# Two feed-forward units multiplied block by block at the entry, and weight conversions and norm sums reordered

## The reference

```python
def rmsnorm(x, g):
    xf = x.astype(jnp.float32)
    y = xf * lax.rsqrt(jnp.mean(xf * xf, axis=-1, keepdims=True) + RMS_EPS)
    return (y * g.astype(jnp.float32)).astype(x.dtype)

def swiglu_2(x, w_gu, w_down):
    gu = x @ w_gu
    gate, up = gu[..., :D_FF], gu[..., D_FF:]
    return (jax.nn.silu(gate) * up) @ w_down
...
        x = x + rmsnorm(m, mix_norm_post[l])
        f = swiglu_2(rmsnorm(x, ffn2_norm_pre[l]), ffn2_w_gu[l], ffn2_w_down[l])
        x = x + 0.5 * rmsnorm(f, ffn2_norm_post[l])
```

## Time and profile before

| what | value |
|---|---|
| median of 3 runs | 3744.84 us (3740.54 to 3745.47) |
| the profiled execution's own time | 3738.52 us |
| its span | 3736.9 us |
| mean granted PE clock | 0.969 |
| start of the entries of stages 3, 5, 7, 9 | 1087.4, 1931.1, 2643.3, 3350.3 us |

### The profile page before, as it was taken

The page is one execution under the profiler, slowest core; times in us unless marked ns, Lnnn a source line. Parts: engine busy times, 40 slices in busy tenths (PEclk is TensorE's granted clock), DMA queues, the critical chain, the costliest instruction groups (busy, mean ns, idle before and its releaser), DMA issues. The chain is left out here.

```text
span 3736.9 us, 45677 instructions
## 1 busy us (share of the span) xinstructions
PE 3495.2 (94%) x18504; PEld 2736.0 (73%) x18510; DVE 2004.4 (54%) x2653; ACT 1123.5 (30%) x1462; POOL 154.0 (4%) x128
## 2 busy tenths in 40 slices
PE   7999999999999999948699999989999989899998
PEld 6887776688878886838468886765788866567886
DVE  5667546522353335897554335697433348954334
ACT  2222334322232223223232223326322232442222
POOL 0000000000000000000000000330000012300000
PEclk8999999999999999969799999999999999999999
DMA  6544221122222222200012222220222221102221
GB/s 229 183 180 170 89 94 45 60 98 101 90 79 98 93 102 76 102 23 4 1 46 101 101 92 80 86 70 15 87 92 99 98 83 68 57 35 92 99 98 71
DMA packets 47213, 325.58 MB, mean 87 GB/s; under 512 B 5232, under 2 KB 5488, under 8 KB 8672
## 3 DMA queue, kind: packets, MB, share of 16 engines
q1 hardware_dynamic: 41792, 290.04, 21.7%
q0 software_dynamic: 5280, 33.52, 2.5%
HBM read 321.44 MB, written 2.10 MB: 87 GB/s over the span
## 5 line engine op out<-in xcount | busy, mean ns | idle before, releaser
L1914 PE MATMUL PS<-HH,WH 128*128 128x512 f32 x2264 | 900.2, 398 | 50.3 <-DVE HL L2300 42.3
L1916 PE MATMUL PS<-HH,WL 128*128 128x512 f32 x2264 | 885.1, 391 | 0.0
L1915 PE MATMUL PS<-HL,WH 128*128 128x512 f32 x2264 | 884.7, 391 | 0.0
L2282 DVE TENSOR_TENSOR WL<-RAW,WH 128x2048 fp32r<-128x2048 f32 x264 | 613.7, 2325 | 502.0 <-ACT WH L2140 496.4
L2140 ACT ACTIVATE WH<-RAW 128x2048 fp32r<-128x2048 f32 x264 | 503.1, 1906 | 327.5 <-PE PS L1916 319.4
L1914 PEld LDWEIGHTS PS<-HH,WH 128*128 128x128 f32 x2264 | 427.2, 189 | 165.8 <-issue 62.3
L1915 PEld LDWEIGHTS PS<-HL,WH 128*128 128x128 f32 x2264 | 427.4, 189 | 90.6 <-issue 4.6
L1916 PEld LDWEIGHTS PS<-HH,WL 128*128 128x128 f32 x2264 | 426.8, 189 | 90.7
L1914 PE MATMUL PS<-AH,WH 128*128 128x512 f32 x1056 | 412.3, 390 | 3.3 <-DVE A L2348 3.0
L1915 PE MATMUL PS<-AL,WH 128*128 128x512 f32 x1056 | 411.4, 390 | 0.0
L1916 PE MATMUL PS<-AH,WL 128*128 128x512 f32 x1056 | 411.3, 389 | 0.0
(11 more groups left out here) (376 smaller groups left out, 3696.8 us busy)
## 6 DMA issues: line engine op xcount, KB each, us to landing
RAW<-in_w SPq DMA_DIRECT2D x264, 1024.0 KB, 4.8
E<-in_ada POOLq DMA_DIRECT2D x28, 1024.0 KB, 5.1
E<-in_ada SPq DMA_DIRECT2D x4, 1024.0 KB, 11.7
G<-in_ada SPq DMA_DIRECT2D x4, 1024.0 KB, 19.3
X<-in_x SPq DMA_DIRECT2D x1, 2048.0 KB, 13.7
out_x<-A SPq DMA_DIRECT2D x8, 256.0 KB, 2.1
G<-in_cos POOLq DMA_DIRECT2D x4, 256.0 KB, 3.3
G<-in_sin POOLq DMA_DIRECT2D x4, 256.0 KB, 3.6
```

What stands on the lines that cost most here:

```text
L1914: nc.tensor.matmul(out, wh, xh, start=start, stop=False)
L1915: nc.tensor.matmul(out, wh, xl, start=False, stop=False)
L1916: return nc.tensor.matmul(out, wl, xh, start=False, stop=stop)
L2282: nc.vector.tensor_tensor(WL[:, w % 2, :], RAW[:, w % 2, :], WH[:, w % 2, :].bitcast(F32), ALU.subtract).then_inc(w_lo, 1)
```

## The change

- Stages 3 and 5: `entry` gives way to `entry_pair`, which multiplies units 0 and 1 together, in an order (unit, chunk) written out; six of the eight norm products go, VectorE adds the squares of seven chunks (six additions, behind the last low half), and `norm_added` stands ahead of the last two blocks. VectorE's conversion of unit 1 moves ahead of chunk 4's term.
- Stages 7 and 9: unit 1's conversion moves ahead of the norm on ScalarE and VectorE; `norm_added` moves from behind unit 0 to the middle of unit 1.
- In the deferred stages PE's wait ahead of unit u >= 2 is for `up_scaled` instead of `act_ready`.
- `keep_clock` has 9 products instead of 6 ahead of stages 3 and 5.
- `add_squares` and `norm_added` take an order; counts of `sq` follow.

```diff
@@ -1960,14 +1960,14 @@
                 if j == n - 1:
                     last.then_inc(stat_done, 1)
 
-            def norm_added():
+            def norm_added(order=ORDER):
 
                 e = t.add("norms")
                 t.add("sq", KD)
                 pe.wait_ge(sq_added, t.add("added"))
-                nc.tensor.matmul(PS[4 + e % 2][:], ONES[:], SQ[:, ORDER[0], :], start=True, stop=False)
+                nc.tensor.matmul(PS[4 + e % 2][:], ONES[:], SQ[:, order[0], :], start=True, stop=False)
                 pe.wait_ge(sq_done, t("sq"))
-                nc.tensor.matmul(PS[4 + e % 2][:], ONES[:], SQ[:, ORDER[-1], :], start=False, stop=True).then_inc(stat_done, 1)
+                nc.tensor.matmul(PS[4 + e % 2][:], ONES[:], SQ[:, order[-1], :], start=False, stop=True).then_inc(stat_done, 1)
 
             def keep_clock(n):
 
@@ -2003,22 +2003,42 @@
                     for c in range(2):
                         last = mm3(PS[c][:], wh[:, KD * c + k, :], wl[:, KD * c + k, :], xh[:, k, :], xl[:, k, :],
                                    n == 0, n == KD - 1)
-                    if n == KD - 1:
+                last.then_inc(w_used, 1)
+
+            def entry_pair(w, s):
+
+                order = [(0, 0), (0, 1), (0, 2), (1, 0), (0, 3), (1, 1), (0, 4), (1, 2), (1, 3), (0, 5), (1, 4), (0, 6), (1, 5),
+                         (0, 7), (1, 6), (1, 7)]
+                pe.wait_ge(x_done, KD * (s - 1) + 2)
+                for u, k in order:
+                    if k == 0:
+                        unit_arrives(w + u)
+                    if u == 0:
+                        pe.wait_ge(hl_done, t("hl") - KD + k + 1)
+                    if (u, k) == (1, 0):
+                        pe.wait_ge(x_done, KD * (s - 1) + 4)
+                    if (u, k) == (1, 6):
+                        norm_added(entry_order(s))
+                    wh, wl = blocks(w + u)
+                    for c in range(2):
+                        last = mm3(PS[2 * u + c][:], wh[:, KD * c + k, :], wl[:, KD * c + k, :], HH[:, k, :], HL[:, k, :],
+                                   k == 0, k == KD - 1)
+                    if k == KD - 1:
                         last.then_inc(w_used, 1)
-                    if post:
-                        norm(part=(n,))
-                if not post:
-                    norm_added()
 
             def ffn(sub, s):
                 w, base = t("w"), t("act_ready")
                 with_ada = plan["ada"] and s == 0
 
-                def gate_up(u, i=0):
+                scaled = t.add("scaled", KF) - KF if deferred(s) else 0
+
+                def gate_up(u, i=0, between=lambda c: None):
                     unit_arrives(w + u, i)
-                    if u >= 2:
+                    if u >= 2 and deferred(s):
+                        pe.wait_ge(up_scaled, scaled + u - 1 + i)
+                    elif u >= 2:
                         pe.wait_ge(act_ready, base + u - 1 + i)
-                    project(w + u, (2 * (u % 2), 2 * (u % 2) + 1), first=u == 0, xs=halves(s))
+                    project(w + u, (2 * (u % 2), 2 * (u % 2) + 1), first=u == 0 and not deferred(s), between=between, xs=halves(s))
                     if with_ada and 2 <= u < KF - 4:
                         ada(ADA_FIRST + u - 2, i)
                     elif with_ada and u >= KF - 4:
@@ -2026,11 +2046,14 @@
                             ada(a - 2)
 
                 t.add("hl", KD)
-                if deferred(s):
+                if deferred(s) and plan["subs"][s - 1]["post"]:
+                    entry_pair(w, s)
+                elif deferred(s):
                     entry(w, s)
+                    gate_up(1, between=lambda c: c == 0 and norm_added(entry_order(s)))
                 else:
                     gate_up(0)
-                gate_up(1)
+                    gate_up(1)
                 with pe.Fori(0, KF - 6, 4) as i:
                     for u in (2, 3, 4, 5):
                         gate_up(u, i)
@@ -2108,7 +2131,7 @@
                     out_projection(K_ORDER.get(sub["kind"], list(range(KD))))
                 if sub["post"]:
                     norm_added()
-                    keep_clock(6)
+                    keep_clock(9 if deferred(s + 1) else 6)
                     t.add("y_evac", len(post_copies(s)))
                 if plan["ada"] and s == 0:
                     pe.wait_ge(y_evac, t("y_evac"))
@@ -2166,6 +2189,8 @@
                     act.wait_ge(x_done, t("x") - KD + n + 1)
                     nc.scalar.activation(halves(s)[0][:, m, :], X[:, m, :], ACT.Copy, scale=col(plan["subs"][s]["pre"], m)).then_inc(hh_done, 1)
                     nc.scalar.activation(SQ[:, m, :], X[:, m, :], ACT.Square).then_inc(sq_done, 1)
+                if not plan["subs"][s - 1]["post"]:
+                    split(t("w") + 1)
                 rsqrt()
 
             def high(src, shift=None, given=0, ready=lambda m: None, order=range(KD), part=range(KD)):
@@ -2265,8 +2290,11 @@
                         split(t("w") + 1)
                         enter(s + 1) if deferred(s + 1) else norm_in(range(KD))
                     else:
-                        enter(s + 1) if deferred(s + 1) else norm_in(ORDER)
-                        split(t("w") + 1)
+                        if deferred(s + 1):
+                            enter(s + 1)
+                        else:
+                            norm_in(ORDER)
+                            split(t("w") + 1)
 
 
         @block.vector
@@ -2405,13 +2433,13 @@
                 t.add("w", DOWN)
                 t.add("ah", DOWN)
 
-            def add_squares(j):
+            def add_squares(j, order=ORDER):
 
                 if j < 1:
                     return
                 dve.wait_ge(sq_done, t("sq") + j + 1)
-                first = SQ[:, ORDER[0], :]
-                ins = nc.vector.tensor_tensor(first, first, SQ[:, ORDER[j], :], ALU.add)
+                first = SQ[:, order[0], :]
+                ins = nc.vector.tensor_tensor(first, first, SQ[:, order[j], :], ALU.add)
                 if j < KD - 2:
                     chain(ins)
                 else:
@@ -2489,7 +2517,7 @@
                         if m in copied:
                             nc.vector.tensor_copy(Y[:, m, :], PS[m][:]).then_inc(y_evac, 1)
                         add_squares(j)
-                    t.add("sq", 2 * KD)
+                    t.add("sq", KD)
                     t.add("y_evac", len(copied))
                     rsqrt()
                     dve.wait_ge(y_evac, t("y_evac"))
@@ -2510,8 +2538,13 @@
                         ready = following
                         if lo and m >= 1:
                             lo(m - 1)
+                        if lo and m == 3:
+                            split(t("w") + 1)
                     if lo:
                         lo(KD - 1)
+                        for j in range(1, KD - 1):
+                            add_squares(j, entry_order(s + 1))
+                    t.add("sq", KD)
                 else:
                     lo = enter(s + 1) if deferred(s + 1) else None
                     for j, m in enumerate(ORDER):
@@ -2532,12 +2566,12 @@
                     dve.wait_ge(ada_used, ADA)
                     modulation(2 * (ADA - ADA_SLOTS), VECTORS * KD)
                 if s + 1 < len(plan["subs"]):
+                    if deferred(s + 1):
+                        rsqrt()
+                        continue
                     if sub["post"]:
                         split(t("w") + 1)
-                    if deferred(s + 1):
-                        rsqrt()
-                    else:
-                        norm_in(plan["subs"][s + 1]["pre"], plan["subs"][s + 1]["shift"])
+                    norm_in(plan["subs"][s + 1]["pre"], plan["subs"][s + 1]["shift"])
                     if not sub["post"]:
                         split(t("w") + 1)
                 elif plan["final"]:
```

## The result

The changed kernel takes 3750.4 us (median of 15 runs, 3747.17 to 3755.53), the kernel before 3741.6 us (15 runs, 3736.09 to 3746.12): ratio 1.0024, 95% interval [1.0016, 1.0031], so 6 to 12 us slower, 9 in the middle. Forecast were +4.5 us and 3749.3 in a range of 3741 to 3757. The time is in the range and the sign is the forecast's. The size is twice the forecast: it lies just beyond the 0.2% up to which I had put 0.75 of the chance, and outside the +1 to +7 us of outcome D, to which I had given 0.65. That the forecast time is off by only 1.1 us is luck: the median of three runs that it starts from, 3744.8, is 3.2 us above that of the fifteen, and the change was forecast 4.3 us too small.

A forecast was written before the change was run, and what follows sets the result against it. TensorE, busy 94%, was taken as the bound. Stages 3 and 5 +5.2, stages 7 and 9 -9.0, cold clock behind the new gaps +8.3: +4.5 us on 3744.84, so 3749.3 us, range 3741 to 3757.

The forecast's parts named there:

- outcome D: The forecast itself as an outcome for the whole kernel: +1 to +7 us, chance 0.65.
- The pair: Stages 3 and 5: unit 2 starts 2.6 us later each, behind a new gap of 6.8 us; together +5.2 us.
- Stages 7 and 9: Their entries: unit 1's conversion hidden, a gap of 4.1 us at unit 2; -3.8 us in stage 7, -5.2 in 9.
- The clock behind the gaps: TensorE's lowered clock after the four new gaps ahead of unit 2: together +8.3 us, bounds 6.1 and 11.9.
- a value between: Clock cost taken behind each 4.1 us gap, in stages 7 and 9: 1.9 us.
- Rival C: Cold clock decides, on the slow side: 2.98 us at each gap gives +8.1, falls in both pairs +11.3; chance 0.2.
- The advice of the Trainium skill: Leave the clock ramp out of the model as under 1% of a typical span; the sum would be -3.8 us.
- Earlier loads: Loads follow the low halves: unit 3's may start some 8 to 10 us sooner, into an idle queue; worth 0.
- the order of banks: New block order in the pair changes banks each block, as unit 0 did already; worth 0.
- the six additions on VectorE: Stages 3 and 5: adding squares takes 4.3 us in idle time of 6.16, done 3.3 us ahead of PE.
- The relaxed wait: Later units wait on the scaled operand, not the product, about 3 us earlier; PE has no gap there, worth 0.
- within 0.2%: Whole time within 0.2% (7.5 us) of the kernel before: chance 0.75.

The follow-up runs named there:

- x3: Changed kernel with unit 2's conversion moved ahead of the norm on ScalarE and VectorE; ratio 0.9977 to the kernel before.
- x9: Changed kernel with the norm products of stages 3 and 5 two blocks earlier; ratio 1.0009 to the kernel before.
- x8: Changed kernel with products that nobody reads laid in the gaps ahead of unit 2, 7 in stages 3 and 5, 4 in 7 and 9; ratio 0.9998 to before.
- x1: Changed kernel with the old entry and 6 clock-keeping products in stages 3 and 5; ratio 0.9994 to the kernel before.
- x10: Changed kernel with 6 clock-keeping products again, in place of 9, ahead of stages 3 and 5; 3749.64 us in one execution.
- x4: Changed kernel with the norm behind unit 0 again in stages 7 and 9, unit 1 still converted early; ratio 0.9993 to the kernel before.
- x12: Kernel before with 6 products that nobody reads added in the middle of stage 3's feed-forward; ratio 1.0017 to the kernel before.
- x7: Changed kernel with old entry and 9 clock-keeping products in stages 3 and 5, norm behind unit 0 in 7 and 9; 3720.75 us, ratio 0.9948 to before.

## Why the prediction was right, and where it was not

- **The pair.** Forecast: U2 at 33.2 us behind the entry's start, behind a gap of 6.8. Measured 33.3 and 6.68. Each step in between held: the conversion of U1 pushes the fourth low half (1101.55 here, 8.36 us behind the first; before, 6.15), the ten blocks run through, the added squares are there (1112.76) 3.3 us ahead of PE. The step that decides, that the chain from Ln to U2's low half isn't edited and only two blocks are left to cover it, is shown from both sides: x3 moves U2's conversion ahead of the chain and the wait for it is gone, x9 moves the chain 2.7 us ahead and the gap shrinks by as much.
- **Stages 7 and 9.** Forecast: a gap of 4.1 at U2 for one of 6.3 at U1, U1's conversion hidden. Measured 3.96 and 3.97. The net gain was forecast at 1.9 and 3.3 us and is 1.9 and 2.2 (means of two traces each).
- **The clock behind the gaps, the term that was mis-sized.** I took 2.25 us behind the long gaps and 1.9 behind the short ones, together 8.3. Against x8 the changed kernel's two traces give about 2.2 behind 6.7 us, and on the mean 2.4 behind 4.0, together 9.2. The gaps of 4.0 in stages 7 and 9 of x1, x9 and x10 widen the sample: their cost is 1.5 to 1.7 or 2.5 to 2.8, in the mean of all ten 2.1, so "a value between" was not far off, and what a single one costs can't be forecast. Without the clock the sum was -3.8; x8, with the gaps filled, has -3.0. The two differences, 0.9 and 0.8, make the entries +6.2 and not +4.5. Rival C, all four at 2.98 and falls in the pairs, is not what happened, though the whole, +9.0, lies in its range; x10 shows that a fall at the pair's start has no price.
- **A row misread.** The 0.68 of stage 9 is the granted clock in the gap itself (3363.00 to 3369.34), not behind it; no term used it.
- **The advice of the Trainium skill** (TensorE: Matmul & The Clock Gate, Part 1: The HAM clock gate) to leave the ramp out would have given -3.8. Filling the gaps took 9 us of entry length and about 10 of the whole: here that term has the size of the whole change. The page also says that the number of slow products at a kernel's start varies from run to run; in the cost of a gap the traces show such a variation too (stage 7: 2.5 and 1.5 us).
- **The rest, some 3 us.** The whole time is 9.0 above before, the entries' sum 6.2; the interval reaches down to 6.0. All seven timed variants of the changed kernel lie 1 to 5 us above their entries' sums, and for x3, x4 and x9 the sum is outside the interval; some of it can be the entries themselves, which come from one trace each (up to 1.1 us per gap of 4.0). The length of the mixers changes with the clock's falls there, by up to 5 us per stage and trace. x12 was meant to tell whether moving the work in time alone does that, and was too weak for it. The fall of stage 1 is another candidate: at 4.1 us, and with one of three traces of before's code against eleven of eleven, it would give 2.7 us on the mean, an estimate from few traces. No run decides between them, so about a third of the measured loss has no shown cause; the other two thirds are the entries.
- **The other steps.** Earlier loads, the order of banks, the six additions on VectorE: nothing in the traces contradicts it. The relaxed wait was worth a few tenths per entry, at the new gap that the change itself makes.
- **Chances.** 0.75 on "within 0.2%" was too much for a forecast of +4.5 with a bound of +8.1, since every term not seen (the clock in stage 1 and in the mixers) adds to the spread.

## What to carry to other kernels

When work is pulled ahead of a reduction, ask what is queued behind that reduction, not only what is in front of it: the pair took 4.2 us of waiting and norm products out of the entry (forecast, and borne out by its rows) and left 2.7 us of work to cover a chain of 9.2. In these entries the place of the norm was set by the longest chain that hangs on it: it goes as early as its input allows, and work that could go ahead of it is kept for behind (x4, x9 and, best of all, x7). And a weight conversion that depends on nothing in that chain shouldn't be queued behind it.

## What was not expected of the hardware

- The cost of a gap in clock hardly follows its length: 2.8 us cost 1.6, 6.7 us cost 1.9 to 2.4, and 4.0 us cost either 1.5 to 1.7 or 2.5 to 2.8, with the same gap in the same entry. Filling all but 0.7 us or less of a gap with products kept the clock at 1.00 in each of the entries of x8.
- The short waits in the pair, five of 0.3 to 0.6 us in 8.3 us, did not bring the clock down in any trace with 9 clock-keeping products. The wait of 1.8 us at the start of stages 7 and 9 did in one entry (stage 7 of x12) and not in the other 27.
- Two executions of one kernel can differ by 4.1 us in a stage because of one fall of the clock. It was absent in two of the fourteen traces, present in twelve, and cost the same each time (stage 1: 307.5 us without it, 311.5 to 311.6 with it, between the same conversions). A difference of two single traces is no measure of a change of this size; the same loop elsewhere repeats to 0.1 us.
